# Alternating the two halves of the array in three attentions of an eight-layer forward pass

## The reference

```
stick: z = q k^T / 8;  w = exp(logsigmoid(z) + sum of log_stay after k);  out = w v
fox:   s = q k^T / 8 + c[t] - c[s];  out = softmax(s, causal) v
nsa:   for each of 4 key groups (4 heads share one group's keys and values):
       cmp: softmax over 15 compressed keys, slc and win: causal softmax over all tokens
       (256 tokens are 4 selectable blocks and shorter than the window, so both see every token)
       out = g0 * o_cmp + g1 * o_slc + g2 * o_win, then @ w_out
```

## Time and profile before

| | |
|---|---|
| runs shown | 1702.99 us median of 3 (1702.11 to 1704.01) |
| profiled execution | 1702.44 us, of it 1700.7 us span |
| mean granted TensorE clock | 0.994 |
| PE busy | 1662.8 us, 98% |
| PEld busy | 1472.0 us, 87% |
| DVE, ACT, POOL busy | 1024.8 us, 809.0 us, 152.2 us |
| transfers | 280 MB read, mean 166 GB/s |

### The profile page before, as it was taken

One profiled execution on the slowest core, in us unless ns is written; L12 is line 12 of the kernel. 1 busy time (PEld: TensorE's weight loads), 2 busy tenths in 40 slices (PEclk: granted clock), 3 DMA queues, 4 the chain that ended last, 5 costly groups with the idle time before them and its releaser, 6 DMA issues.

```text
span 1700.7 us, 25652 instructions
## 1 busy us (share of the span) xinstructions
PE 1662.8 (98%) x10390; PEld 1472.0 (87%) x10390; DVE 1024.8 (60%) x1044; ACT 809.0 (48%) x990; POOL 152.2 (9%) x117
## 2 busy tenths in 40 slices
PE   7999999999999999999999999989999999999998
PEld 6888887888889888888888998867998899889887
DVE  6454666654457645576545687755755577566564
ACT  6343567544345534455434556344534355444432
POOL 1000122300002000012000131221000001100000
PEclk9999999999999999999999999898999999999999
DMA  7545442264553654545454443312445434325551
GB/s 306 193 164 207 159 173 75 101 254 171 199 196 124 225 195 176 207 173 204 167 203 167 155 184 125 123 50 75 170 177 193 177 143 182 122 100 198 190 181 50
DMA packets 39626, 282.18 MB, mean 166 GB/s; under 512 B 4416, under 2 KB 4544, under 8 KB 5760
## 3 DMA queue, kind: packets, MB, share of 16 engines
q1 hardware_dynamic: 39168, 279.59, 44.7%
q0 software_dynamic: 384, 1.51, 0.2%
HBM read 280.04 MB, written 1.05 MB: 165 GB/s over the span
## 4 chain that ended last, share of the span: by engine, by line
PE 91%; DVE 4%; ACT 2%; POOL 1%; issue 1%; DMA 1%; POOLq 0%; SPq 0%; DVEq 0%; ACTq 0%
PE ps L359 28%; PE ps L362 27%; PE ps L363 27%; PE ps L557 1%; DVE w_lo L1666 1%; DMA raw<-weights 1%; PE ps L973 1%; PE ps L966 1%; ACT w_hi L1203 0%; POOL arena L2384 0%; PE ps L658 0%; ACT arena L1500 0%; PE ps L929 0%; PE ps L832 0%; PE ps L488 0%
## 5 line engine op out<-in xcount | busy, mean ns | idle before, releaser
L1666 DVE TENSOR_TENSOR w_lo<-raw,w_hi 128x2048 fp32r<-128x2048 f32 x264 | 601.4, 2298 | 160.4 <-ACT w_hi L1203 160.4
L1203 ACT ACTIVATE w_hi<-raw 128x2048 fp32r<-128x2048 f32 x264 | 496.7, 1906 | 49.3 <-DMA raw<-weights 49.2
L359 PE MATMUL ps<-w_hi,hT_hi 128*128 128x512 f32 (+1 forms) x984 | 383.6, 390 | 13.1 <-DVE hT_lo L1678 11.2
L363 PE MATMUL ps<-w_hi,hT_lo 128*128 128x512 f32 (+1 forms) x984 | 375.2, 381 | 0.0
L362 PE MATMUL ps<-w_lo,hT_hi 128*128 128x512 f32 (+1 forms) x984 | 374.5, 381 | 0.0
L359 PE MATMUL ps<-hT_hi,w_hi 128*128 128x256 f32 x984 | 284.2, 289 | 2.6 <-DVE hT_lo L2294 1.5
L362 PE MATMUL ps<-hT_lo,w_hi 128*128 128x256 f32 x984 | 278.6, 283 | 0.0
L363 PE MATMUL ps<-hT_hi,w_lo 128*128 128x256 f32 x984 | 278.6, 283 | 0.0
L359 PEld LDWEIGHTS ps<-w_hi,hT_hi 128*128 128x128 f32 x984 | 186.0, 189 | 47.6 <-DVE w_lo L1666 11.4
L363 PEld LDWEIGHTS ps<-w_hi,hT_lo 128*128 128x128 f32 x984 | 185.7, 189 | 36.0
L362 PEld LDWEIGHTS ps<-w_lo,hT_hi 128*128 128x128 f32 x984 | 186.3, 189 | 32.1 <-issue 0.7
(11 more groups left out here) (269 smaller groups left out, 1863.4 us busy)
## 6 DMA issues: line engine op xcount, KB each, us to landing
raw<-weights SPq DMA_DIRECT2D x264, 1024.0 KB, 4.8
X<-x SPq DMA_DIRECT2D x2, 512.0 KB, 7.1
out<-X SPq DMA_DIRECT2D x4, 256.0 KB, 2.1
arena<-p POOLq DMA_DIRECT2D x2, 256.0 KB, 5.1
arena<-counts POOLq DMA_DIRECT2D x1, 512.0 KB, 5.2
arena<-nsa_tables POOLq DMA_DIRECT2D x1, 448.0 KB, 6.5
const<-constants SPq DMA_DIRECT2D x1, 427.0 KB, 9.9
cols<-parameters SPq DMA_DIRECT2D x1, 213.5 KB, 2.5
```

Source lines behind the costliest of these rows:

```text
L359: mm = nc.tensor.matmul(dst, a_hi, b_hi, start=start, stop=False, skip_group_check=True)
L363: return nc.tensor.matmul(dst, a_lo, b_hi, start=False, stop=stop, skip_group_check=True)
L1203: nc.scalar.activation(unit_cols(w_hi, u, 0, UNIT), raw[:, r * UNIT:(r + 1) * UNIT], ACT.Copy).then_inc(hi_done.sem, 1)
L1666: nc.vector.tensor_tensor(unit_cols(w_lo, u, 0, UNIT), raw[:, r * UNIT:(r + 1) * UNIT], f(unit_cols(w_hi, u, 0, UNIT)), ALU.subtract).then ...
```

## The change

Every attention's matmuls on a half of the array are issued so that lower and upper half take turns.

- `PAIRED_HALVES` is the new order of stick's and fox's scores: A of a lower head beside B tiles of upper heads and the other way about, so that the two never write the same bank at once. The semaphore, now `odd_done`, is raised by the last upper B tile, and the first lower B tile waits for it.
- `weighted` in stick and fox goes by pairs of heads, tile by tile, lower and upper in turn. nsa's `weighted` keeps its order.
- In nsa the heads are renumbered on the host (columns of the gates, rows of `w_out`) and `q_of`, `k_of`, `v_of` and `cmp_keys` follow: a job is now a pair of heads of **two** key groups, one on each half. Head `r` has bank `a + r`: columns 0 to 255 its A tile, 256 to 383 its B tile; the two mask matmuls have the same size, one per bank. In a cmp job heads alternate between banks `a` and `a + 1`.
- On DVE, one instruction becomes two for the cmp mask (L2081), one becomes four for the compressed values (L2151), and maxima and gates only read in another pattern. ACT's exponentials read the other columns.

```diff
+PAIRED_HALVES = [(0, False), (2, True), (3, True), (1, False), (2, False), (0, True), (3, False), (1, True)]
@@ stick scores(g)
-                    for s in range(HG):
+                    for s, later in PAIRED_HALVES:
                         h = HG * g + SLOT_HEAD[s]
-                        nc.tensor.matmul(A(3, s, 0, 256), head(KT, h, 0, P), head(QT, h), start=True, stop=True)
-                        if s == 2:
-                            pe.wait_ge(*even_done.due(me))
-                        mm = nc.tensor.matmul(bank(5, s * P, P), head(KT, h, P, P), head(QT, h, P, P), start=True, stop=True)
-                        if s == 1:
-                            mm.then_inc(even_done.sem, 1)
+                        if later:
+                            if s == 0:
+                                pe.wait_ge(*odd_done.due(me))
+                            mm = nc.tensor.matmul(bank(5, s * P, P), head(KT, h, P, P), head(QT, h, P, P), start=True, stop=True)
+                            if s == 3:
+                                mm.then_inc(odd_done.sem, 1)
+                        else:
+                            nc.tensor.matmul(A(3, s, 0, 256), head(KT, h, 0, P), head(QT, h), start=True, stop=True)
@@ stick weighted(g); fox scores(g) and weighted(g) change in the same way
-                    for s in range(HG):
-                        j = SLOT_HEAD[s]
-                        h = HG * g + j
...
+                    for pair in range(HG // 2):
+                        for tile in range(TT):
+                            for j in (2 * pair, 2 * pair + 1):
+                                h, s = HG * g + j, SLOT_HEAD[j]
...
@@ nsa
-                r = DH * (h // HG % 2)
+                r = DH * (h % 2)
+            def group_of(h):
+                return h // (2 * HG) * 2 + h % 2
@@ nsa scores(n), cmp
-                                mm = nc.tensor.matmul(bank(a, (qt * HG + j) * CPAD, CPAD), q_of(HG * g + j, qt * P), cmp_keys(g), start=True, stop=True, skip_group_check=True)
+                                mm = nc.tensor.matmul(bank(a + j % 2, (qt * 2 + j // 2) * CPAD, CPAD), q_of(HG * g + j, qt * P), cmp_keys(HG * g + j), start=True, stop=True, skip_group_check=True)
@@ nsa scores(n), slc and win
+                    h = HG * g + 2 * pair
                     for r in range(2):
-                        h = HG * g + 2 * pair + r
-                        nc.tensor.matmul(bank(a, r * 256, 256), q_of(h, P), k_of(br, h, 256), start=r == 0, stop=False, skip_group_check=True)
-                        nc.tensor.matmul(bank(a + 1, r * P, P), q_of(h, 0), k_of(br, h, P), start=r == 0, stop=False, skip_group_check=True)
+                        nc.tensor.matmul(bank(a + r, 0, 256), q_of(h + r, P), k_of(br, h + r, 256), start=True, stop=False, skip_group_check=True)
+                    for r in range(2):
+                        nc.tensor.matmul(bank(a + r, 256, P), q_of(h + r, 0), k_of(br, h + r, P), start=False, stop=False, skip_group_check=True)
...
+                    for r in range(2):
+                        mm = nc.tensor.matmul(bank(a + r, P, 256).rearrange("p (t k) -> p t k", t=TT), IDENT_M, mask, start=False, stop=True, skip_group_check=True)
```

More of the change, by code:

```diff
@@ L198, in turned_of, with two_banks @@
             return at(o, 512), at(o + 512, 256)
+        def two_banks(b):
+            return ps[:, b * 512:(b + 2) * 512].rearrange("p (r x) -> p r x", r=2)
         def cmp_turned(thread):
@@ L311, in network_kernel @@
         aside_done = S("aside_done")
-        act_step, dve_step, pool_step, even_done = S("act_step"), S("dve_step"), S("pool_step"), S("even_done")
+        act_step, dve_step, pool_step, odd_done = S("act_step"), S("dve_step"), S("pool_step"), S("odd_done")
         split = {"act": 0, "dve": 0}
@@ L797, in scores @@
                         nc.tensor.matmul(bank(2, s * P, P), pick, FORGET[:, 0:P], start=s == 0, stop=False, skip_group_check=True)
-                    for s in range(HG):
+                    for s, first in PAIRED_HALVES:
                         h = HG * g + SLOT_HEAD[s]
[L800 to L805, removed]
+                        if first:
+                            if s == 0:
+                                pe.wait_ge(*odd_done.due(me))
+                            mm = nc.tensor.matmul(bank(2, s * P, P), head(QT, h, 0, P), head(KT, h, 0, P), start=False, stop=True, skip_group_check=True)
+                            if s == 3:
+                                mm.then_inc(odd_done.sem, 1)
+                        else:
+                            nc.tensor.matmul(A(0, s, 0, 256), head(QT, h, P, P), head(KT, h, 0, 256), start=False, stop=True, skip_group_check=True)
                     mm.then_inc(s_full.sem, 1)
@@ L826, in weighted @@
                     tA, tB = at(3072, 1024), at(ACT_AT, 512)
[L827 to L833, removed]
+                    for pair in range(HG // 2):
+                        for tile in range(TT):
+                            for j in (2 * pair, 2 * pair + 1):
+                                h, s = HG * g + j, SLOT_HEAD[j]
+                                r, o = DH * (h % 2), 3 * 512 + pair * TOKENS
+                                v = at(QKV + 4096 + tile * DM + h * DH, DH)
+                                if tile == 0:
+                                    nc.tensor.matmul(ps[r:r + DH, o:o + TOKENS], v, tA[:, s * 256:(s + 1) * 256], start=pair == 0, stop=False, skip_group_check=True)
+                                else:
+                                    mm = nc.tensor.matmul(ps[r:r + DH, o + P:o + TOKENS], v, tB[:, s * P:(s + 1) * P], start=False, stop=True, skip_group_check=True)
                     mm.then_inc(hT_full.sem, 1)
@@ L885, in v_of @@
                 def v_of(br, h, tok):
-                    return at(NSA_KV + (0 if br == "slc" else 512) + tok * 256 + h // HG * DH, DH)
+                    return at(NSA_KV + (0 if br == "slc" else 512) + tok * 256 + group_of(h) * DH, DH)
                 def unit(i, b, mid={}):
@@ L2080, in maxima @@
                         m3 = K("cmp_mask").rearrange("p (t c) -> p t c", t=TT)
-                        step(nc.vector.tensor_tensor(S.rearrange("p (t h c) -> p t h c", t=TT, h=HG), bank(a, 0, 256).rearrange("p (t h c) -> p t h c", t=TT, h=HG),
-                                                     m3.unsqueeze(2).broadcast_to((P, TT, HG, CPAD)), ALU.add))
+                        for qt in range(TT):
+                            ins = nc.vector.tensor_tensor(S[:, qt * P:(qt + 1) * P].rearrange("p (r j c) -> p r j c", r=2, j=2),
+                                                          two_banks(a)[:, :, qt * 2 * CPAD:(qt + 1) * 2 * CPAD].rearrange("p r (j c) -> p r j c", j=2),
+                                                          m3[:, qt:qt + 1, :].unsqueeze(1).broadcast_to((P, 2, 2, CPAD)), ALU.add)
+                            if qt == TT - 1:
+                                step(ins)
                         m, rows = nmax[:, 8:16], S.rearrange("p (a d) -> p a d", a=cmp_rows)
@@ L2102, in weights @@
                         step(nc.vector.reciprocal(coef, total))
-                        step(nc.vector.tensor_tensor(c3, c3, gates[:, :, HG * g:HG * (g + 1), 0], ALU.mult))
+                        step(nc.vector.tensor_tensor(coef.rearrange("p (t r j) -> p t r j", t=TT, r=2), coef.rearrange("p (t r j) -> p t r j", t=TT, r=2),
+                                                     gates[:, :, HG * g:HG * (g + 1), 0].rearrange("p t (j r) -> p t r j", r=2), ALU.mult))
                         step(nc.vector.tensor_tensor(c3, c3, K("cmp_valid").unsqueeze(2).broadcast_to((P, TT, HG)), ALU.mult))
@@ L2591 @@
     qs = [q[:, 256 * i:256 * (i + 1)] for i in range(4)]
-    gates = np.concatenate([w[:, 2560:], np.zeros((DM, P - 3 * HEADS), np.float32)], axis=1)
+    head = np.array([4 * (2 * s + r) + 2 * j + t for s in range(2) for t in range(2) for j in range(2) for r in range(2)])
+    gates = w[:, 2560:].reshape(DM, HEADS, 3)[:, head].reshape(DM, 3 * HEADS)
+    gates = np.concatenate([gates, np.zeros((DM, P - 3 * HEADS), np.float32)], axis=1)
     w1 = v["nsa_cmp_w1_2"][0]
@@ L2595 @@
         units += as_units(chunks(part))
-    units += out_units(v["nsa_w_out_2"][0]) + mlp_units(v["mlp_w_up_2"][0], v["mlp_w_down_2"][0])
+    units += out_units(v["nsa_w_out_2"][0].reshape(HEADS, DH, DM)[head].reshape(DM, DM)) + mlp_units(v["mlp_w_up_2"][0], v["mlp_w_down_2"][0])
     w = v["fox_w_in_2"][0]
```

38 lines of the change are left out of this document (21 added, 17 removed).

## The result

The kernel after runs in 1680.59 us (median of 4 runs, 1680.39 to 1681.42), the one before beside it in 1702.55 us (1700.70 to 1704.01): ratio 0.9876, 95% interval 0.9864 to 0.9887. The forecast was 1680.0. The profiled execution took 1681.42 us, its span is 1679.6 us, the mean granted clock 0.997.

What follows compares the result with a forecast made beforehand. PE, busy 98% of the span, was taken as the bound, except in nsa's steady rounds. Stick 5.7, fox 7.6, nsa 7.25, clock 3.4, less 1.0, took 22.95 us off 1702.44; with 0.55 for the median, 1680.0 us, range 1673 to 1691.

Steps and rivals of the forecast that it cites:

- The price of a matmul on half the array: Scores on PE: 128-column matmul 0.22 us, 256-column 0.44, a head 0.66, 0.09 at each end; both halves run at once.
- the rival of shared loads: The two halves' weight loads cannot run at once, a pass costs 0.107 whichever half: 12.8 us saved, 1690; chance 0.10.
- the estimate from the page of the Trainium skill: nsa's cmp scores: about 62 ns sequencer cost per matmul makes 16 passes 0.99 us, not 0.86.
- Stick: Stick's stage: three scores jobs save 1.20 us each (3.6), weights jobs 2.1, 5.7 in all; one job's saving becomes wait.
- Fox: Fox's stage: four scores jobs save 1.20 us each (4.8), weights jobs 2.8, 7.6 in all.
- The lump of 0.7 for late places: 0.7 us lost where POOL already ends just before PE asks: fox's transposes, stick's last weights jobs.
- nsa: nsa's stage: 3.3 from jobs between projection steps, cmp jobs 1.7, 0.85 and 1.4: 7.25 us, clock apart.
- The ring: nsa jobs 7 to 13: a 5.0 us ring through POOL's product stands, saves nothing; PE's wait grows from 0.77 to about 1.4.
- its 1.4 for job 17: End of nsa: job 17's scores run at 1.2 GHz, cost double and save about 1.4 us.
- The clock: nsa: the 6.8 us at half clock from 1082.6, put down to cmp scores, goes: 3.4 us saved, bounds 0 and 3.4.
- The slower rival: nsa: the clock stays low, PE becomes the bound, each round takes 2.1 us longer: up to 1708.6; chance 0.03.
- The sum: Whole kernel: stick 5.7, fox 7.6, nsa 7.25, clock 3.4, less 1.0: 22.95 us saved.

Runs made afterwards that it cites:

- before_again: The kernel before, unchanged, in one more profiled execution: 1701.60 us.
- p_stick: The kernel before with only stick's new order of scores and weights: 1697.17 us, ratio 0.9967.
- a_swap: The kernel after with an nsa job's two products exchanged, DVE taking the 512 columns and POOL the 256: 1678.96 us, ratio 0.9861.

## Why the prediction was right

**The price of a matmul on half the array** held everywhere: scores job 1.50 us forecast, 1.51 measured; nsa's 0.84 and 0.86; weights jobs two and four slots; cmp, called the least sure, 1.04 and 1.01. By that the rival of shared loads (1.04 for nsa's scores, 1.89 for cmp) is out. So is the estimate from the page of the Trainium skill ("TensorE: Matmul & The Clock Gate", Part 1), 0.99 us for the 16 passes of a cmp job: 1.01 less the 0.18 at the ends leaves 0.83. The page gives its 62 ns for a core whose hardware decode is off, a condition that the prediction left out, so the trace does not say that the figure is wrong.

**Stick** 5.7 forecast, 5.68 measured, with the first job's saving lost in L664's wait: forecast 2.6, measured 2.67.

**Fox** 7.6 forecast, 6.61 measured. The failed step is "ACT, DVE and POOL start there when PE ends a job or a projection unit, so they move with PE". For job 0 DVE is busy throughout with weight splits, does not move, and turns the 1.2 us into the new wait of L824 (1.3). The lump of 0.7 for late places named fox's transposes and so covered part of it, but put it down to POOL, not to DVE.

**nsa** 7.25 and 3.4 for the clock, less 0.3; 9.91 and 10.76 measured. The ring held: rounds 5.0, the wait of a round 1.4. The scores of jobs 0 to 3 gave 2.6 (2.64 forecast), and 1.2 of that went again at two places where DVE's splits and the rotation (L947) were late. It came back behind job 9, where 3.75 us were won and 2.25 forecast (its 1.4 for job 17 is 1.3 by its own price, 2 x 0.66): 0.65 of it in one round of the steady part (1125.86 in the record), whose savings were put at nothing and where PE had waited 0.67 us for DVE's `hT_lo` and no longer does; the rest at the end of the stage, along with a last fall of 6.8 instead of 10.2 us.

**The clock** is the term that was mis-sized. That the fall behind the cmp jobs goes is shown; but 3.4 us was the price of one long fall in one execution. In three other profiles it is half as long, so 1.7 seems the usual price, and against before_again the new nsa wins 8.1 to 8.9 us. What made up for that, the gains behind job 9, the forecast had not named; so it is in part luck that the total came out this close.

How much of these gains comes from the last fall, shorter by 3.4 us, is not shown. From the transposes at 1148.36 to the weights job at 1168.65 (record) is 20.3 us in before, 20.1 in before_again and 19.8 in p_stick, whose nsa code is the same and whose last fall is 6.8 us too: there it was worth about 0.3. In the new order the same stretch is 18.2 and 18.0, and 17.2 in a_swap with 3.4 us of fall. Nor do denser cmp scores take this last fall away, though the prediction read both long falls as standing "right behind cmp scores": it is in all thirteen profiles.

**The slower rival** had PE less busy and the clock low for it. PE was busy in only 77% of 1094.8 to 1135.6, and the clock stood at 1.00.

**The sum**: 22.95 forecast from the record, 21.14 by the spans; the spans include the program's start, which came 0.9 later, and the 0.2 of the other stages. The three attentions alone give 22.2: fox is 1.0 and nsa, with its 0.3 for the added work, 0.4 short of their terms, and the lump of 0.7 stood for about half of that. The added instructions show nowhere by themselves (DVE busy 1024.7 us, before 1024.8). By the medians it is 21.96.

## What to carry over

Where operands fill half of PE's rows or columns, alternate the halves instruction by instruction: on this kernel a scores job fell from 2.70 to 1.51 us with no other work changed. Then ask of each saving whether the next engine moves with PE; where it is busy without a gap (DVE ahead of fox's first transposes) or where a ring does not hold PE's work (nsa's rounds), the saving turns into a wait one for one. Take a price for a fall of the clock from several executions. And before halving an engine's work, look at what its neighbour does beside it: a_swap's product seems to have lost to DVE most of what it won in columns.

## What the runs showed of the hardware

- The first pass on an idle half started together with the pass four places ahead of it in the program, and so ahead of three that waited for the other half; of eight only the last four overlapped (1.01, 1.48 and 1.89 us for the same 16 passes in three orders).
- Two halves cost one another nothing: a pair of 32-column passes with its loads took (1.01 - 0.18) / 8 = 0.10 us, a single pass before 0.107. In both traces the starts inside a job lie 0.112 us apart; the 0.107 has a part of the ends in the 0.18.
- The clock fell to 1.2 GHz once behind a stretch with PE busy 3.30 of 3.30 us (1079.2 to 1082.5, cmp scores) and once behind one with 1.28 of 3.40 us, and it held 2.4 GHz at 77% busy for 40.8 us; the same kernel had the same fall for 6.8 us in one execution and 3.4 in another.
- POOL took 1.12 us for a product of 256 columns and 1.28 for one of 512, each beside a DVE product (0.69 and 0.42 us) that had started 0.04 us before; from that one's end it is 0.47 and 0.90 us. A POOL sum of 256 columns with DVE idle took 0.74 us.
